# A router product with the weights as the fixed operand, and the expert masks of all tiles made ahead of the shares

## What is computed

```python
logits = (h @ router_w).astype(jnp.float32)        # h: 384 x 1024, router_w: 1024 x 8
top_v, top_i = lax.top_k(logits, MOE_TOP_K)        # 2 of 8
gates = jax.nn.softmax(top_v, axis=-1)
combine = jnp.sum(jax.nn.one_hot(top_i, N_EXPERTS) * gates[..., None], axis=-2)
for e in range(N_EXPERTS):
    y = y + combine[..., e:e + 1] * swiglu(h, w1[e], w3[e], w2[e])
```

## Time and profile before

| | |
|---|---|
| median of three runs | 1384.89 us (1383.79 to 1385.86) |
| the profiled execution | 1383.07 us, span 1381.2 us, mean granted clock 0.950 |
| busy share of the span | PE 91%, DVE 65%, ACT 55%, POOL 20% |
| the norm's products and the router, from the first turn to the gathers | 821.8 to 859.1 us of the span |
| the expert jobs | from 866.4 us to the end |

### The profile page before, as it was taken

How to read it: one execution, slowest core, us unless ns; L and a number is a source line. 1 busy time by engine, 2 the same in 40 slices (tenths; PEclk the granted TensorE clock), 3 DMA queues, 4 the chain that set the end, 5 groups by cost and what they waited for, 6 DMA issues and landing times.

```text
span 1381.2 us, 19756 instructions
## 1 busy us (share of the span) xinstructions
PE 1261.1 (91%) x7731; PEld 1111.0 (80%) x7731; DVE 892.2 (65%) x1130; ACT 758.6 (55%) x1113; POOL 281.8 (20%) x227
## 2 busy tenths in 40 slices
PE   5986899899999998998969889999999999999895
PEld 3884567799889986995647788988989889889793
DVE  1538867453433344765766435888889789799686
ACT  3657755542323234433464334777777777777673
POOL 0158950100110012000060010030321312303103
PEclk9998999999999998998979786999999999999998
DMA  9752985153444345313417130999899899899881
GB/s 313 195 189 89 299 289 190 54 167 101 145 127 133 100 145 168 123 62 100 140 40 240 58 126 16 309 329 322 285 334 336 262 348 315 288 338 322 276 297 74
DMA packets 180249, 277.68 MB, mean 201 GB/s; under 512 B 8528, under 2 KB 107352, under 8 KB 180152
## 3 DMA queue, kind: packets, MB, share of 16 engines
q1 hardware_dynamic: 179064, 272.80, 59.7%
q0 software_dynamic: 1088, 3.56, 0.8%
HBM read 274.02 MB, written 2.31 MB: 200 GB/s over the span
## 4 chain that ended last, share of the span: by engine, by line
PE 73%; DVE 10%; issue 9%; ACT 5%; POOL 1%; SPq 1%; DMA 0%; DVEq 0%; ACTq 0%; POOLq 0%
PE psB L2056 5%; PE psB L2058 5%; PE psB L2057 5%; PE psB L1551 5%; PE psB L1552 5%; PE psB L1553 4%; PE psA L2056 4%; PE psA L2058 4%; PE psA L2057 4%; PE psB L1791 2%; PE psB L1790 2%; PE psB L1789 2%; PE psA L1551 2%; PE psA L2007 2%; PE psA L1552 2%
## 5 line engine op out<-in xcount | busy, mean ns | idle before, releaser
L2686 DVE TENSOR_TENSOR Wl<-raw,Wh 128x1408 fp32r<-128x1408 f32 (+2 forms) x144 | 247.3, 1740 | 57.4 <-ACT Wh L1451 56.7
L2119 DVE TENSOR_TENSOR Wl<-raw,Wh 128x2048 fp32r<-128x2048 f32 (+4 forms) x64 | 133.8, 2096 | 144.0 <-ACT Wh L1093 143.9
L1451 ACT CAST Wh<-raw 128x1408 fp32r<-128x1408 f32 (+2 forms) x144 | 196.9, 1375 | 27.9 <-PE psA L2058 14.5
L1093 ACT CAST Wh<-raw 128x2048 fp32r<-128x2048 f32 (+4 forms) x64 | 110.0, 1724 | 111.2 <-PE psB L1791 64.2
L2056 PE MATMUL psA<-Wh,hTh 128*128 128x352 f32 x360 | 118.5, 329 | 0.7 <-ACT hTl L1457 0.7
L2058 PE MATMUL psA<-Wh,hTl 128*128 128x352 f32 x360 | 116.9, 325 | 0.0
L2057 PE MATMUL psA<-Wl,hTh 128*128 128x352 f32 x360 | 116.4, 323 | 0.0
L1551 PE MATMUL psB<-Wh,hTh 128*128 128x256 f32 (+2 forms) x356 | 104.9, 295 | 6.9 <-DVE zq L2494 4.1
L989 POOL TENSOR_TENSOR yc<-yc,work 128x414 f32<-128x414 f32 x90 | 100.9, 1143 | 45.2 <-ACT work L1192 41.0
L1552 PE MATMUL psB<-Wl,hTh 128*128 128x256 f32 (+2 forms) x356 | 104.1, 292 | 0.0
L1553 PE MATMUL psB<-Wh,hTl 128*128 128x256 f32 (+2 forms) x356 | 104.0, 292 | 0.0
(11 more groups left out here) (365 smaller groups left out, 3379.7 us busy)
## 6 DMA issues: line engine op xcount, KB each, us to landing
raw<-in_l_moe_w SPq DMA_DIRECT2D x108, 704.0 KB, 5.5
raw<-in_l_ada_w SPq DMA_DIRECT2D x40, 1024.0 KB, 5.3
raw<-in_l_ffn_w SPq DMA_DIRECT2D x28, 1024.0 KB, 5.3
raw<-in_l_moe_w SPq DMA_DIRECT2D x27, 768.0 KB, 6.0
gate_b<-in_l_moe_w SPq DMA_DIRECT2D x18, 768.0 KB, 7.0
gate_b<-in_l_moe_w SPq DMA_DIRECT2D x18, 704.0 KB, 5.8
raw_tail<-in_l_moe_w SPq DMA_DIRECT2D x18, 704.0 KB, 5.6
raw<-in_l_w_in SPq DMA_DIRECT2D x11, 1024.0 KB, 5.6
```

The costliest lines, as they stand in the source:

```text
L1093: act.copy(hi_of(u), raw_of(u)).then_inc(hi_ready, 1)
L1451: act.copy(half_of(Wh, h), raw_half(h)).then_inc(half_hi, 1)
L2119: dve.tensor_tensor(lo_of(u), raw_of(u), hi_of(u).bitcast(F32), ALU.subtract).then_inc(lo_ready, 1)
L2686: dve.tensor_tensor(half_of(Wl, h), raw_half(h), half_of(Wh, h).bitcast(F32), ALU.subtract).then_inc(half_lo, 1)
```

## The change

The router's hi and lo weights are laid side by side in `Wh`, 16 columns a feature group. This pair is the fixed operand; 384 tokens move through it. Rows 0 to 7 of the output bank collect hi x hi and hi x lo tokens, rows 8 to 15 lo x hi. The result lies with logits on partitions and tokens along the bank, so ACT copies its 16 x 384 values to `hf[0:16, 1, :]`, and PE multiplies each tile of it by two stacked 8 x 8 units (`C_PAIR`), which adds the two halves and brings rows back. DVE then makes both one-hots of all tiles, their sum as mask with its signal, and only then the shares and `comb`.

```diff
-C_END = 908
+C_PAIR = 908
+C_END = 916
+    c[0:2 * NE, C_PAIR:C_PAIR + NE] = np.concatenate([np.eye(NE), np.eye(NE)])
+        sel = sb("sel", [P, 2, NT, NE])
+        def router_pair():
+            kt, n = units[base["router"]][1:]
+            at = base["router"] % S * SLOT
+            return Wh[:, at:at + 2 * kt * n].rearrange("p (k r n) -> p k r n", k=kt, r=2)
+        def split_views(u):
+            if u == base["router"]:
+                return by_k(raw_of(u), u), router_pair()[:, :, 0, :], router_pair()[:, :, 1, :]
+            return raw_of(u), hi_of(u), lo_of(u)
-                takes("router", b=NT)
+                takes("router", b=2)
 # ACT
             step(base["router"])
+            g = first["router"]["B"]
+            act.wait_ge(psB_full, g + 1)
+            act.copy(hf[0:2 * NE, 1, :], psB[g % 3][0:2 * NE, 0:TOK]).then_inc(psB_free, 1)
             table_of(ACT.Exp)
             act.wait_ge(router_in, 1)
             act.activation(rt[:, 4:7], rt[:, 0:3], ACT.Exp).then_inc(logit_e, 1)
 # PE
+            def router_products(k):
+                g = first["router"]["B"]
+                if k == 0:
+                    pe.wait_ge(lo_ready, base["router"] + 1)
+                    free_b(g)
+                pair = router_pair()[:, k, :, :].rearrange("p r n -> p (r n)")
+                both, high = psB[g % 3][0:2 * NE, 0:TOK], psB[g % 3][0:NE, 0:TOK]
+                if k == KD - 1:
+                    pe.matmul(high, pair[:, 0:NE], hTl[:, k, :], start=False, stop=False)
+                last = pe.matmul(both, pair, hTh[:, k, :], start=(k == 0), stop=(k == KD - 1))
+                if k < KD - 1:
+                    pe.matmul(high, pair[:, 0:NE], hTl[:, k, :], start=False, stop=False)
+                else:
+                    last.then_inc(psB_full, 1)
-            norm(1, 1, rows_products(base["router"], first["router"]["B"]))
+            norm(1, 1, router_products)
+            g = first["router"]["B"] + 1
+            pe.wait_ge(psB_free, g)
+            for t in range(NT):
+                last = pe.matmul(psB[g % 3][:, t * NE:(t + 1) * NE], hf[0:2 * NE, 1, t * P:(t + 1) * P],
+                                 cst[0:2 * NE, C_PAIR:C_PAIR + NE], start=True, stop=True)
+            last.then_inc(psB_full, 1)
 # DVE
+            dve.wait_ge(psB_full, g + 1)
             for t in range(NT):
+                b = psB[g % 3][:, t * NE:(t + 1) * NE]
                 link(dve.max(mx8[:, t, :], b))
+                ins = dve.max_index(ix8[:, t, :], mx8[:, t, :], b)
+            ins.then_inc(psB_free, 1)
+            dve.tensor_tensor(rt[:, 0:3], mx8[:, :, 1], mx8[:, :, 0], ALU.subtract).then_inc(router_in, 1)
+            dve.wait_ge(psB_free, g + 1)
             link(dve.tensor_copy(ix8f[:, :, :], ix8[:, :, :]))
+            iota = cst[:, C_IOTA:C_IOTA + NE]
+            each = iota.unsqueeze(1).to_broadcast([P, NT, NE])
+            for c in range(2):
+                link(dve.tensor_tensor(sel[:, c, :, :], each, ix8f[:, :, c:c + 1].to_broadcast([P, NT, NE]),
+                                       ALU.is_equal))
+            dve.tensor_tensor(mask[:, :, :], sel[:, 0, :, :], sel[:, 1, :, :], ALU.add).then_inc(mask_ready, 1)
+            dve.wait_ge(mask_ready, 1)
             dve.wait_ge(logit_e, 1)
             link(dve.tensor_scalar(rt[:, 8:11], rt[:, 4:7], 1.0, None, ALU.add))
             link(dve.reciprocal(rt[:, 12:15], rt[:, 8:11]))
             link(dve.tensor_tensor(rt[:, 16:19], rt[:, 12:15], rt[:, 4:7], ALU.mult))
-            for t in range(NT):
-                link(dve.tensor_scalar(rt[:, 40:48], iota, ix8f[:, t, 0:1], None, ALU.is_equal))
-                link(dve.scalar_tensor_tensor(out=mask[:, t, :], in0=iota, scalar=ix8f[:, t, 1:2], in1=rt[:, 40:48],
-                                              op0=ALU.is_equal, op1=ALU.add))
...
-            nothing().then_inc(mask_ready, 1)
+            for c in range(2):
+                share = rt[:, 12 + 4 * c:15 + 4 * c].unsqueeze(2).to_broadcast([P, NT, NE])
+                link(dve.tensor_tensor(sel[:, c, :, :], sel[:, c, :, :], share, ALU.mult))
+            link(dve.tensor_tensor(comb[:, :, :], sel[:, 0, :, :], sel[:, 1, :, :], ALU.add))
```

More of the change, by code:

```diff
@@ L510, in trunk_step @@
             last_group[base["lat", 1] + 2 + j] = ("B", first["lat"]["B"] + 2 * NT + 4 * j + 3)
-        last_group[base["router"]] = ("B", first["router"]["B"] + NT - 1)
+        last_group[base["router"]] = ("B", first["router"]["B"])
         full = {"A": psA_full, "B": psB_full, "part": part_used}
@@ L1092, in split_to @@
                         act.wait_ge(full[group], g + 1)
-                    act.copy(hi_of(u), raw_of(u)).then_inc(hi_ready, 1)
+                    act.copy(split_views(u)[1], split_views(u)[0]).then_inc(hi_ready, 1)
                 splits[0] = max(splits[0], last + 1)
@@ L2118, in split_to @@
                     dve.wait_ge(hi_ready, u + 1)
-                    dve.tensor_tensor(lo_of(u), raw_of(u), hi_of(u).bitcast(F32), ALU.subtract).then_inc(lo_ready, 1)
+                    w, wh, wl = split_views(u)
+                    dve.tensor_tensor(wl, w, wh.bitcast(F32), ALU.subtract).then_inc(lo_ready, 1)
                 splits[0] = max(splits[0], last + 1)
@@ L2627, in _ @@
             step(base["router"])
-            g = first["router"]["B"]
-            dve.wait_ge(psB_full, g + NT)
+            g = first["router"]["B"] + 1
+            dve.wait_ge(psB_full, g + 1)
             for t in range(NT):
-                b = psB[(g + t) % 3][:, 0:NE]
+                b = psB[g % 3][:, t * NE:(t + 1) * NE]
                 link(dve.max(mx8[:, t, :], b))
-                dve.max_index(ix8[:, t, :], mx8[:, t, :], b).then_inc(psB_free, 1)
-            dve.wait_ge(psB_free, g + NT)
+                ins = dve.max_index(ix8[:, t, :], mx8[:, t, :], b)
+            ins.then_inc(psB_free, 1)
+            dve.tensor_tensor(rt[:, 0:3], mx8[:, :, 1], mx8[:, :, 0], ALU.subtract).then_inc(router_in, 1)
+            dve.wait_ge(psB_free, g + 1)
             link(dve.tensor_copy(ix8f[:, :, :], ix8[:, :, :]))
-            dve.tensor_tensor(rt[:, 0:3], mx8[:, :, 1], mx8[:, :, 0], ALU.subtract).then_inc(router_in, 1)
+            iota = cst[:, C_IOTA:C_IOTA + NE]
[5 more added lines that the diff above has]
+            dve.wait_ge(mask_ready, 1)
             dve.wait_ge(logit_e, 1)
@@ L2640, in _ @@
             link(dve.tensor_tensor(rt[:, 16:19], rt[:, 12:15], rt[:, 4:7], ALU.mult))
-            iota = cst[:, C_IOTA:C_IOTA + NE]
-            for t in range(NT):
-                link(dve.tensor_scalar(rt[:, 40:48], iota, ix8f[:, t, 0:1], None, ALU.is_equal))
-                link(dve.scalar_tensor_tensor(out=mask[:, t, :], in0=iota, scalar=ix8f[:, t, 1:2], in1=rt[:, 40:48],
-                                              op0=ALU.is_equal, op1=ALU.add))
[L2646 to L2649, removed]
-            nothing().then_inc(mask_ready, 1)
+            for c in range(2):
+                share = rt[:, 12 + 4 * c:15 + 4 * c].unsqueeze(2).to_broadcast([P, NT, NE])
+                link(dve.tensor_tensor(sel[:, c, :, :], sel[:, c, :, :], share, ALU.mult))
+            link(dve.tensor_tensor(comb[:, :, :], sel[:, 0, :, :], sel[:, 1, :, :], ALU.add))
             g = first["tables"]["B"]
```

## The result

The changed kernel takes 1370.44 us (1368.97 to 1371.56, four runs), the kernel before 1384.92 beside it (1383.79 to 1385.86): ratio 0.989, 95% interval 0.9876 to 0.9903. Of the 4.4 us between the two, 2.5 lie by the traces in the stage that the forecast was about (from the norm's first turn to the first gather), and the other 1.9 outside it, where the forecast had nothing. The sign and the mechanism held; one term was missing and two were too small. The profiled execution of after took 1370.85 us, span 1369.0.

A forecast was written before the change was run, and what follows sets the result against it. The router stretch was taken as a bare chain of engines, PE full at 1.2 GHz. Norm 9.0, minus 2.0 back to rows, plus 1.85 masks gave 8.9; halfway to 11.4 is 10.1: 1384.89 - 10.1 = 1374.8 us, range 1371.5 to 1379.5.

The forecast's parts named there:

- eight more columns of `cst` and the new tile `sel`: Wider constants and a new tile for the router: the same instructions, off the path, costing nothing.
- Norm: Router's norm: steps of 1.20 us instead of 2.48, last bank full at 833.95 instead of 843.05, gain 9.0 us.
- the second branch: Router stage with the clock back at 829 and kept: last bank full at 833.4, gain 11.4 us.
- Way back to rows: Between full bank and transposes: ACT copy, handovers, three fp32 matmuls; 2.0 us given back at 1.2 GHz, 1.6 at 2.4.
- Masks: On DVE: masks 2.3 us after the logits instead of 6.45, worth exactly the 1.85 us that PE idled.
- Counts: Mask matmuls on PE: counts come 2.84 us later instead of 3.24 if the clock is back and kept.
- Transposes to counts: Token transposes on PE: until 840.7 at 1.2 GHz; at 2.4 GHz ACT's copies pace them, ending near 838.6.
- (a): Router stage: the clock does not come back before the masks' end; gain 7.8 us, time 1377.1, chance 0.23.
- (b): Norm's products: the narrow fixed operand costs 0.64 us a matmul; gain 5 to 6 us, time 1379.5, chance 0.05.
- (c): Expert jobs: PE and DMA are near full, so the gain doesn't reach the end; time 1384.9, chance 0.05.
- (d): Gathers and first job: PE enters them at 1.2 GHz after more waits, so slower; time 1387.7, chance 0.02.
- The prediction's case of 1.85 us: Mask matmuls of the kernel before: clock at 0.55 after PE waited 1.85 us, cited as waits putting the clock back.

The follow-up runs named there:

- the run of the old masks: The changed kernel with the old loop making masks and shares tile after tile: 1374.63 us, ratio 0.9917.
- masks first: The kernel before with only `sel` and the new mask code, router products as before: 1385.08 us, ratio 0.9991.
- the last of the late exponentials: The changed kernel plus 20 unused matmuls ahead of the norm and ACT's exponential behind the third token copy, late tiles unmoved: 1368.53 us, ratio 0.9872.
- the run with the late exponential at 184064: The changed kernel plus 20 unused matmuls ahead of the norm, exponential behind the third token copy, `gTh` moved to 184064: 1369.7 us, ratio 0.9890.

## Why the prediction was wrong

**The step that failed** is "eight more columns of `cst` and the new tile `sel`: the same instructions, off the path, nothing". They issue nothing, and they moved `gTh` and `mTh` from 160 to 128 past a multiple of 256 bytes, where `Wh` stands. In the kernel before that is worth 6.0 us by itself, 5.7 with plain unused bytes, and nothing when an unused tile of 96 bytes puts them elsewhere. In the changed kernel it is less sure: 2.1 to 3.0 us by medians whose intervals overlap, 3.2 in the two stretches of single traces that hold the groups (2.0 + 1.2), 5.8 in the summed durations. It is also the step that took the result out of the range: with the tiles put back it was 1372.55. No row of the trace of before could show it; the diff could, as everything declared behind the wider `cst` and the new `sel` moves.

**The sum for the stage was too small**: 12.6 us measured, 10.1 forecast. Its terms:

- Norm. Steps 1.28 us (0.49 for the turns, 0.47 and 0.32 for the pair), forecast 1.20 (0.56 and 2 x 0.32). The forecast had two branches, the last bank full 12.18 us after the first turn with the clock at 0.50, 11.6 with the clock back at 829. It was 834.71 + 0.34 - 823.43 = 11.62: the clock came back in 831 to 833 and the second branch's number held. That is in part luck: the clock came back later than the 829 of that branch, the last turn stood 8.49 us after the first (831.92 in that trace) against 8.38 by the slow steps, and it was the chain from there to the full bank that was shorter, 3.13 us instead of 3.80. I took the middle of both branches, and this cost 1.3 of the 2.5 us that the stage was off.
- Way back to rows. Copy 0.47 (0.48 forecast); from the full bank to the first transpose 836.37 - 835.05 = 1.32 us, where the sum for 2.4 GHz had 0.06 + 0.48 + 0.06 + 0.89 = 1.49. Right in kind.
- Masks. 2.33 us after the logits (2.3), PE doesn't wait for them, and 1.85 is gone. Right. POOL's memsets beside them show as one slow conversion, 0.49 instead of 0.18, within the cover. It took 0.49 to 0.50 in all nine profiles in which POOL's last memset ran beside it, and ended with that memset each time (within 0.04); it took 0.18 in the nine in which the memset was over.
- Counts. 2.18 us instead of 3.24, forecast at best 2.84. The 0.148 of an entry that I read off was a mean over both clock levels. At 1.00 the entries cost (841.18 - 839.92)/12 = 0.105 and (841.85 - 841.18)/6 = 0.112, where 841.85 is the start of the second transposes. This term was mis-sized by 0.66 us.
- Transposes to counts. ACT's table load stands ahead of the copies, as forecast, and PE waits 0.55 for a bank. The counts start 16.49 us after the first turn where the second branch had 16.83, 0.3 us better. From the counts' reader to the gathers 0.2 more came. So 1.3 + 0.7 + 0.3 + 0.2 make the 2.5.

**The rivals.** (a) fell in the stage of the changed kernel, though the clock is not settled: a second execution of it lost it among the transposes at the same sum. (b) fell: a step of 1.28 has no room for two passes. (c) fell: the jobs start 11 us earlier and end earlier, with PE and DMA as full as before, as this window shows beside the earlier trace rows.

```profile
859.00:989.00 130.00, 126.75 (x742) 118.03 (x742) 112.98 (x96) 98.19 (x102) 26.04 (x12) 1.00 0.93 313
```

(d) has the right place and a small price: gathers at 0.50 in three of the experiments, 1.5 to 2.1 us each time. In the run of the old masks a wait of 2.84 us stands ahead of it; in the other two (masks first, and the last of the late exponentials) the last wait ahead of it is one of 1.65 us, which the changed kernel has too and passed at 1.00. The prediction's case of 1.85 us is therefore weak evidence that waits do it. The clearest wait of this kernel is the one of 3.91 us ahead of the norm's first turn (823.43 above): the clock fell in it, the first steps ran at 0.50, and with 20 matmuls in it they ran at 1.00. The Trainium skill ("TensorE: Matmul & The Clock Gate", "HAM oscillation — how this bites in real kernels") describes a kernel whose waits for DMA put the clock back each time. The wait of 3.91 us agrees with it; for the losses behind shorter waits these runs show no rule.

**What stays open**: why operands that stand alike are faster, and why 256-column matmuls show nothing of it. The runs show it for 512 columns of weights past fixed tokens (396 to 389 ns) and for 384 columns of tokens past fixed weights (339 to 335); they don't show which memory access waits for which. How the gain divides between SwiGLU and jobs was not tried by itself, as both share one start.

## What to carry to other kernels

A tile or a column that nothing reads can move every tile declared after it: before a gain or a loss is put down to an edit, run the kernel of before with the new declarations alone. Compare the mean of the large matmul groups that the edit does not touch; if it differs, look at where their operands start. In this kernel the fast place, for the 384- and 512-column matmuls, was where moving and fixed tile start alike past a multiple of 256 bytes. Where a narrow stream is turned round so that few instructions move many columns, price what follows at both clock levels, from entries measured at each.

## What was not expected of the hardware

- Place: SwiGLU's 512-column fp32r matmuls start 0.227 us apart (389 ns a record) where both operands start alike past a multiple of 256 bytes, 0.231 to 0.237 (394 to 396) where they don't; 5.4 to 6.0 us of 1386 in the kernel before, for 990 such matmuls (3 x 132 + 3 x 198). The Trainium skill, "SBUF — State Buffer", section "Operand start alignment", speaks of an operand's start as a matter of legality and says of its runs "these runs timed nothing"; here the start has a price.
- A fixed operand of 16 and of 8 columns costs the stream of 384 nearly the same (828.57 - 828.38 = 0.19 and 828.74 - 828.57 = 0.17 us at 2.4 GHz, in the timeline of the run with the late exponential at 184064).
- Plain fp32 entries of 8 columns: 0.105 to 0.112 us at 2.4 GHz, 0.213 at 1.2.
- Where the clock is lost is not the same in two executions of one kernel: the changed one kept it among the transposes in one (3.55 us to the counts) and lost it there in the other (4.29), after the logits had come 0.62 us sooner; the stage took 24.66 and 24.79 us.
